# The residual's input moved from GpSimd to VectorE, upward tiles in seven banks, and a new order of the first mixers

## The reference

```python
# first block, 2 layers; mod = silu(c) @ ada_w + ada_b gives shift, scale, gate for each of 3 steps
y = swiglu(modulate(x, shift, scale), w13, w2)                # D_FF = 2816
x = layer_norm(ALPHA * x + 0.5 * (1 + gate) * y, g, b)
y = token_mixer(modulate(x, ...), w_in, w_out, ...)           # gated delta rule, MoBA attention, mLSTM
x = layer_norm(ALPHA * x + (1 + gate) * y, g, b)
y = swiglu(...)                                               # a second feed-forward
x = layer_norm(...)
# second block, 2 layers
y = hybrid mixer(x)       # differential attention, bidirectional HGRN2, attention over a memory
x = layer_norm(alpha * x + y)
y = feed-forward with a convolution of width 3 over the tokens before its gate
x = layer_norm(alpha * x + y)
```

## Time and profile before

| | |
|---|---|
| median of 3 runs | 2046.53 us |
| the profiled execution | 2047.77 us |
| its span, first to last instruction | 2045.9 us |
| TensorE busy | 1977.9 us, 97% |
| VectorE busy | 1580.9 us, 77% |
| ScalarE busy | 1050.9 us, 51% |
| GpSimd busy | 302.4 us, 15% |
| mean granted TensorE clock | 0.995 |
| read from memory | 404 MB, 199 GB/s over the span |

### The profile page before, as it was taken

The page is one execution under the profiler, slowest core; times in us unless marked ns, Lnnn a source line. Parts: engine busy times, 40 slices in busy tenths (PEclk is TensorE's granted clock), DMA queues, the critical chain, the costliest instruction groups (busy, mean ns, idle before and its releaser), DMA issues.

```text
span 2045.9 us, 39790 instructions
## 1 busy us (share of the span) xinstructions
PE 1977.9 (97%) x17036; PEld 1836.6 (90%) x17036; DVE 1580.9 (77%) x2078; ACT 1050.9 (51%) x1451; POOL 302.4 (15%) x255
## 2 busy tenths in 40 slices
PE   7999999999999999999999999999999999999998
PEld 7999889989998998889889989887899899878996
DVE  6699898676987787787676649986798489858974
ACT  4544365545434543554554436665666375746652
POOL 0200031012000200302021002710110027001100
PEclk9999999999999999999999999999999999999999
DMA  9889832235995788422255662342455533334552
GB/s 379 338 339 371 335 117 91 104 125 205 350 345 223 259 338 339 165 103 84 105 192 218 250 235 108 132 157 89 159 207 185 206 137 134 125 109 164 218 192 81
DMA packets 60096, 409.88 MB, mean 200 GB/s; under 512 B 6865, under 2 KB 6865, under 8 KB 13329
## 3 DMA queue, kind: packets, MB, share of 16 engines
q1 hardware_dynamic: 53712, 384.85, 50.5%
q0 software_dynamic: 5920, 22.07, 3.2%
q10 hardware_dynamic: 288, 0.42, 0.1%
HBM read 404.17 MB, written 3.15 MB: 199 GB/s over the span
## 4 chain that ended last, share of the span: by engine, by line
PE 70%; DVE 17%; ACT 5%; issue 3%; POOL 3%; DMA 2%; POOLq 0%; DVEq 0%; SPq 0%; ACTq 0%
PE ps L764 11%; PE ps L766 11%; PE ps L765 11%; PE ps L823 7%; PE ps L825 6%; PE ps L824 6%; DVE l L646 6%; PE ps L1820 2%; PE ps L808 2%; ACT h L631 2%; PE ps L670 2%; PE ps L809 2%; PE ps L810 2%; DMA w<-in_stream 2%; PE ps L883 1%
## 5 line engine op out<-in xcount | busy, mean ns | idle before, releaser
L646 DVE TENSOR_TENSOR l<-w,h 128x2048 fp32r<-128x2048 f32 (+1 forms) x293 | 682.9, 2335 | 127.2 <-ACT h L631 126.8
L631 ACT CAST h<-w 128x2048 fp32r<-128x2048 f32 (+1 forms) x293 | 555.7, 1902 | 343.0 <-PE ps L825 145.9
L764 PE MATMUL ps<-xh,h 128*128 128x256 f32 x2368 | 667.6, 282 | 12.9 <-DVE sa L1469 6.3
L765 PE MATMUL ps<-xl,h 128*128 128x256 f32 x2368 | 659.8, 279 | 0.0
L766 PE MATMUL ps<-xh,l 128*128 128x256 f32 x2368 | 659.7, 279 | 0.0
L764 PEld LDWEIGHTS ps<-xh,h 128*128 128x128 f32 x2368 | 447.9, 189 | 20.5 <-issue 10.1
L765 PEld LDWEIGHTS ps<-xl,h 128*128 128x128 f32 x2368 | 447.0, 189 | 2.2 <-issue 2.2
L766 PEld LDWEIGHTS ps<-xh,l 128*128 128x128 f32 x2368 | 447.0, 189 | 0.0
L823 PE MATMUL ps<-h,hh 128*128 128x512 f32 x528 | 207.0, 392 | 0.0
L824 PE MATMUL ps<-l,hh 128*128 128x512 f32 x528 | 205.5, 389 | 0.0
L825 PE MATMUL ps<-h,hl 128*128 128x512 f32 x528 | 205.5, 389 | 0.0
(11 more groups left out here) (435 smaller groups left out, 3154.8 us busy)
## 6 DMA issues: line engine op xcount, KB each, us to landing
w<-in_stream SPq DMA_DIRECT2D x363, 1024.0 KB, 5.0
GB<-in_vec POOLq DMA_DIRECT2D x20, 512.0 KB, 5.9
gate<-in_vec POOLq DMA_DIRECT2D x6, 512.0 KB, 4.1
w<-in_stream SPq DMA_DIRECT2D x4, 512.0 KB, 4.8
memf<-in_memT SPq DMA_DIRECT2D x2, 512.0 KB, 5.3
xf<-in_xT POOLq DMA_DIRECT2D x1, 1024.0 KB, 10.0
kv<-mk POOLq DMA_DIRECT2D x2, 512.0 KB, 4.7
kv<-mv POOLq DMA_DIRECT2D x2, 512.0 KB, 8.2
```

The lines of the kernel that those rows point to most:

```text
L631: e.copy(part(k.H, m, z), k.W[n % NW][:, 0:z]).then_inc(k.hi_done, 1)
L646: e.tensor_tensor(part(k.L, m, z), k.W[n % NW][:, 0:z], part(k.H, m, z), SUB).then_inc(k.lo_done, 1)
L764: p.matmul(P[:, 0:T], H[:, r, o], xh[:, r, :], start=r == 0, stop=False)
L765: p.matmul(P[:, 0:T], H[:, r, o], xl[:, r, :], start=False, stop=False)
```

## The change

It has four parts.

1. **The residual's input.** `pool_x` is gone, and VectorE makes all of them with `dve_x`: 28 operations more on VectorE, 28 fewer on GpSimd. In the feed-forwards one operation follows each of the upward chunks 5 to 8 of the stage; in `mix1` a new letter `x` in VectorE's string places them. Whoever reads the result now waits on VectorE's semaphore.
2. **New strings** `ORDER1` for TensorE, VectorE and ScalarE in the first mixers, and one wait more on TensorE for GpSimd's `psel` in MoBA.
3. **Seven banks.** Upward tiles of the feed-forwards go round banks 0, 1, 2, 4, 5, 6, 7 after the first four, whose banks depend on the stage before. Bank 3 stays for the sums of the modulation weights. The downward products wait for up to seven banks. In the second mixers the `h` group goes round four banks, 4, 5, 7, 6.
4. **The third chunk's lower part first.** In `ffn2` the call before the loop asks for one chunk more.

```diff
+UPS = (0, 1, 2, 4, 5, 6, 7)
...
     def x_done(self, s):
-        return (self.lv if STAGES[s + 1][0] == "mix2" else self.lg)(s, "x_in", 3)
+        return self.lv(s, "x_in", 3)
...
             if kind in ("ffn1", "ffn2"):
+                lead = (0, 1, 2, 3) if STAGES[s - 1][0] in ("mix1", "mix2") else (0, 1, 6, 7)
                 for u in range(4 * NC2):
-                    self.tile_bank[first + u] = 3 if u == 3 else u % 3
+                    self.tile_bank[first + u] = lead[u] if u < 4 else UPS[u % 7]
...
-def pool_x(k, g, s):
...
-    k.freed.update({k.tile_bank[pe.t - n]: k.evac[pe.t - n] for n in (3, 2, 1)})
+    k.freed.update({k.tile_bank[pe.t - n]: k.evac[pe.t - n] for n in range(7, 0, -1)})
...
 def dve_ffn1(k, v, s, feed):
-    F = ffn_at(s)
+    F, x_in = ffn_at(s), dve_x(k, v, s)
...
         dve_ada(k, v, m)
+        if s > 1 and m in ups(s)[4:8]:
+            next(x_in)
...
 def dve_ffn2(k, v, s, feed):
-    feed.lo(ups(s)[0] + 1)
+    x_in = dve_x(k, v, s)
+    feed.lo(ups(s)[0] + 2)
...
+        if m in ups(s)[4:8]:
+            next(x_in)
...
 ORDER1 = dict(
-    dve=("twrr tww t trr trrw t tggwgg tgw t t t t trw twgbggr t tggggwgbgb t tgggb tgggwgggbbb tgggw t tw tgmg tmggbbgg "
...
+    dve=("t twwrrxw tx trrwrr t txxg tgw t trg tgg tw tw tgwbggr t t tg tgggwgggbbgb tgg tgggwggbb tgw tg tbwggg tmg "
...
+    p.wait_ge(*k.rg(l, "psel", 2))
...
-    interleave(ORDER1["dve"], t=each(tile, tiles1(l)), w=more(feed.lo, feed, ORDER1["dve"].count("w")), r=dve_rows(k, v, l), g=dve_gdn(k, v, l),
+    interleave(ORDER1["dve"], x=dve_x(k, v, s), t=each(tile, tiles1(l)), w=more(feed.lo, feed, ORDER1["dve"].count("w")), r=dve_rows(k, v, l), g=dve_gdn(k, v, l),
...
+HMIX, DMIX = (4, 5, 7, 6), (7, 6)
...
-    pe_mix(k, p, l, k.ho, (4, 5), hv_(l, "on", 3), hp, hv_, 4, keep=7)
+    pe_mix(k, p, l, k.ho, HMIX, hv_(l, "on", 3), hp, hv_, 4, keep=7)
```

More of the change, by code:

```diff
@@ L507, in norm_steps @@
             if not last:
-                (self.lv if STAGES[s + 1][0] == "mix2" else self.lg).add(s, x_in=4)
+                self.lv.add(s, x_in=4)
     def down_table(self):
@@ L1103, in pool_norm @@
             g.tensor_tensor(k.XL[:, 2 * i:2 * i + 2, :], k.tmp[:, i % 3, :, :], k.XH[:, 2 * i:2 * i + 2, :], SUB).then_inc(lg.sem, 1)
-RESID = 4
-def pool_x(k, g, s):
[L1111 to L1124, removed]
 def dve_x(k, v, s):
@@ L1607 @@
 ORDER1 = dict(
-    pe=("tr t t t trr t trgrrrr tgg t t tg t tggg tgb t tggbb tggg tg tbgggb tgbgggggg tggb tbg tbgmg t tmgggg tggmgg "
-        "tg tggmg t tgmg tmgg tmgmmmmgggboomm"),
-    dve=("twrr tww t trr trrw t tggwgg tgw t t t t trw twgbggr t tggggwgbgb t tgggb tgggwgggbbb tgggw t tw tgmg tmggbbgg "
-        "tgwgwg t tgmgg tgwm tgggg tgm tgwgwgmggbmmmmmwmwm t"),
-    act=("twwr t trr trrrw t tw trrgw tg tgw t tg t tgw tggg t t tgwgbgbwggggg t tbgggbgwg tggbwgb tggbg tb tbggw tgggw "
-        "tgmwgg tmgmg tmmggwg tgm tmmgmgw tgggg t tgwgbmmmwm"),
+    pe=("r trr t t trr t t tgrrr tg tg t t t tggg tgbg t tggbb tggggg t tbg tgggbggbgg tgb tbgg tgbggmg t tmggg tggmgg "
+        "tgg tggm t tgmg tmggg tgmmmmggoobmmm"),
+    dve=("t twwrrxw tx trrwrr t txxg tgw t trg tgg tw tw tgwbggr t t tg tgggwgggbbgb tgg tgggwggbb tgw tg tbwggg tmg "
+        "tmgggwggbg t tg tm t t twgmwgggggbgmwggwgmgggmmbm tmmwmwm t"),
+    act=("tww t tr trrwrr trrw t trgw t tggw t tg t tgw tgg tgggw tb t twgggb tgggbgggwg tgbbgwgbb tgg tg tbbggwgg tgwg "
+        "tgwggm tgmmggmm tg tgmmmw tgg tmwggggg t tgwgbmwmmm"),
 )
@@ L2867, in dve_hgrn @@
     yield
-    dve_mix(k, v, l, (4, 5), ha, hv_, k.mixh2, k.mixl2, k.htmp, 4, lambda i: k.COL[:, ROW["hnorm"] + l:ROW["hnorm"] + l + 1], 4)
+    dve_mix(k, v, l, HMIX, ha, hv_, k.mixh2, k.mixl2, k.htmp, 4, lambda i: k.COL[:, ROW["hnorm"] + l:ROW["hnorm"] + l + 1], 4)
     yield
@@ L2921, in act_hgrn @@
     e.wait_ge(k.tile_pe, TILE[FIRST["win2", l, MIX2[-1]] + 1])
-    act_mix(k, e, l, (4, 5), hp, ha, k.mixh2, 4, lambda i: k.COL[:, ROW["hnorm"] + l:ROW["hnorm"] + l + 1], 4)
+    act_mix(k, e, l, HMIX, hp, ha, k.mixh2, 4, lambda i: k.COL[:, ROW["hnorm"] + l:ROW["hnorm"] + l + 1], 4)
     yield
@@ L3017, in pe_diff @@
     yield
-    pe_mix(k, p, l, k.do, (7, 6), dv_(l, "on", 1), dp, dv_, 4, keep=18)
+    pe_mix(k, p, l, k.do, DMIX, dv_(l, "on", 1), dp, dv_, 4, keep=18)
     yield
@@ L3104, in dve_diff @@
     yield
-    dve_mix(k, v, l, (7, 6), da, dv_, k.mixh2, k.mixl2, k.dtmp, 0, lambda i: k.COL[:, ROW["dnorm"] + l:ROW["dnorm"] + l + 1], 4)
+    dve_mix(k, v, l, DMIX, da, dv_, k.mixh2, k.mixl2, k.dtmp, 0, lambda i: k.COL[:, ROW["dnorm"] + l:ROW["dnorm"] + l + 1], 4)
     yield
@@ L3163, in act_diff @@
     e.wait_ge(k.tile_pe, TILE[FIRST["win2", l, MIX2[-1]] + 1])
[L3164 removed]
+    act_mix(k, e, l, DMIX, dp, da, k.mixh2, 0, lambda i: k.COL[:, ROW["dnorm"] + l:ROW["dnorm"] + l + 1], 4)
     yield
```

4 lines of the change are left out of this document (removed).

## The result

The changed kernel takes 2038.66 us (median of 9 runs, 2032.08 to 2044.83) against 2049.28 us (9 runs, 2044.29 to 2054.34) of the kernel before beside it: a ratio of 0.9944, 95% interval 0.9927 to 0.9961. That is 0.56% or some 11 us less; forecast were 5.2 us less, 2041.3 us in a range of 2034.0 to 2048.5. (The forecast started from a median of 2046.5 us of three runs; the nine beside the changed kernel give 2049.3.) Run again later it gave 0.9947 (0.9924 to 0.9970). The profiled execution took 2037.63 us, its span 2035.8 us, with a clock of 0.997.

What follows compares the result with a forecast made beforehand. TensorE, busy 1977.9 of 2045.9 us, was taken as the bound. Terms +2.2 (first mixers), -2.6 (ffn2), -2.8 (pace), -1.2 (s3), -0.8 (second mixers) sum to -5.2 us: 2041.3 us against 2046.5, range 2034 to 2048.5.

Steps and rivals of the forecast that it cites:

- First mixers: +1.1 each: s2 and s5: low clock +1.7 less the Dk wait 0.6 makes each slower by 1.1 us, +2.2 together.
- Behind `RB`: First mixers: a gap up to 5.4 us at RB, then low clock costing 1.7 us; the Dk wait of 0.6 goes.
- the balance of -0.03: First mixers: VectorE's savings and added operations ahead of RB nearly cancel, so RB stays at 292.0 us.
- `Dk` went as forecast: First mixers: TensorE's wait for Dk, 0.6 us each, goes.
- `ffn2`: -1.3 each: s8 and s10: bank waits go, TensorE runs 1.2 to 1.3 us ahead, then meets lower parts; -2.6 us together.
- Pace: -2.8: Slow matmul stretches in s8 and s10 cost 5.6 us; drawn anew, half of that is won.
- the fast pace everywhere: Rival, chance 0.12: the other half of the 5.6 us and s1's slow stretch also go, -5.2 more, 2036.1 us.
- s3: -1.2: s3: the wait for gate, 1.2 us, goes because VectorE gets back 2.15 us shortly before.
- Second mixers: -0.8: s7 and s9: four banks remove the htmp waits, but TensorE then waits for epp; -0.8 us for both.
- overloaded in `ffn2`: Rival, chance 0.11: four x operations per stage make lower parts late and stall TensorE; 2055.7 us, likelier 2051.
- the gains turn into waits for lower parts: Rival, chance 0.20: VectorE's order limits ffn2 and s3, their terms and the pace are 0; 2047.9 us, half 2044.5.
- The mixers gain too: Rival, chance 0.18: no low clock behind RB and RB sooner; first mixers -0.6 to -4.3 us each, 2030.5 to 2038.

Runs made afterwards that it cites:

- a_pool: Changed kernel with the residual's input back on GpSimd in all stages, letters x gone from VectorE's string: 1.0006 of the kernel before.
- a_nofill: Changed kernel without the filler of 48 products in each first mixer: 0.9954 of the kernel before.
- a_poolffn: Changed kernel with the residual's input back on GpSimd in the feed-forwards only: 0.9974 of the kernel before.
- a_banks3: Changed kernel with the feed-forwards' upward tiles in three banks again: 0.9952 of the kernel before.
- a_hmix2: Changed kernel with two banks again for the h group of the second mixers: 0.9959 of the kernel before.
- a_break: Changed kernel with one useless product behind each upward chunk of ffn2 from the fifth on: 0.9951 of the kernel before.
- b_banks7_lo: Kernel before with seven banks in the feed-forwards and the third lower part first in ffn2, nothing else: 0.9988 of the kernel before.
- b_dvex: Kernel before with the residual's input on VectorE in all stages, letters x in the old string and the psel wait: 1.0004 of the kernel before.
- a_again: Changed kernel run again unaltered in a later batch: 0.9947 of the kernel before.

## Why the prediction was right, and where it was not

**The time.** 2038.7 us lies in the range, on its lower side; the gain is twice the forecast. That it lies in the range is in part luck and the range's width: the first mixers' term had the wrong sign, 6.7 us off in both together, that of `ffn2` was too small by half, and those of s3 and of the second mixers did not come.

**First mixers: +1.1 each was forecast, -2.0 to -2.5 each came.** The step that failed is "Behind `RB`": a gap of up to 5.4 us with the low clock after it. In its place the runs showed a gap of 1.4 us there and no fall of the clock. The step itself exists: `a_pool` shows the fall behind a gap of 3.8 us, `a_nofill` the fall and its 1.7 us behind 6.6 us. What was wrong were the two arrivals. The end of the filler came 3.1 us earlier in the stage (filler from 872.19 before and 868.89 after, with the stage's start 0.2 us apart), not the 4.8 us that 3.1 and 1.7 make, because ScalarE's `A` still holds the bank of the third chunk's first tile (1.44 us), a wait that had been hidden behind the lower part's. And the balance of -0.03 failed: `RB` came 2.3 us earlier, 1.6 of it from the locked `A` operation that I had not counted. So the wait for `RB` became 0.6 + 3.1 - 2.3 = 1.4 us. I had looked for GpSimd's effect in the long instructions alone, and a short one can lose as much. That the wait would move to `RB` and not vanish was right, with 1.4 us instead of 3 to 5. `Dk` went as forecast.

**`ffn2`: -1.3 each forecast, -2.4 came.** In the seven profiles that have all four parts in `ffn2` and no more than one interruption in it, s8 takes 187.4 or 190.0 us and s10 182.7 or 185.2, as the last 67 us of the upward tiles are fast or slow: 2.6 us, worked out and measured (67 x 0.038). Before, with both slow, they took 192.4 and 187.7. So 2.4 us each are waits (before, 3.2 us in each stage behind `sa`), the rest of the 5.0 is the draw. The mechanism was named, VectorE's lower parts, but the end of the lock was set against the new operations as if it were only a cover; it was the gain itself: 4.1 to 5.0 us of waits for lower parts come back in s8 with GpSimd's operations (`a_poolffn`, `a_pool`), and three banks cost nothing that could be measured (`a_banks3`).

**Pace: -2.8.** In the profile the slow stretches of the feed-forwards' upward tiles fell from 288 to 161 us, worth 4.8 us, which looks like the other rival ("the fast pace everywhere") half come true. But the second profile of the same kernel has 422 us of them. Probably it largely averages out in the medians: the mixers' 4.5 us and the waits of `ffn2`, 4.8, make 9.3 of the 11 us without it. With s1 it accounts for the distance between the two profiles, and probably for much of the runs' spread of over 12 us. A term that is drawn belongs into the range, not into the sum. Two readings behind the term were rough: the counts in a window include products cut by its edges, so that 112.4 and 116.7 ns are 113.3 and 117.8 from start to start, and the slow stretch at the end of s8 is 67.6 us, not 76.

**s3: -1.2 forecast, none.** The wait for `gate` was 2.2, 2.6 and in other runs 0.3 to 3.2 us. The DMA share from 540 to 590 us is above 0.9 before and after, and the sums `acc` follow the chunks as they come; that faster VectorE work waits there for the stream fits this, but no run tests it. Where the wait was 2.8 and 3.2 us (`a_hmix2`, `a_break`), the clock fell to 0.50 as well and s3 took 198.3 us. **Second mixers: -0.8 forecast, none:** the wait went over to `epp` whole (3.1 for 3.4 us), so VectorE's chain was the limit entirely. In the profile s7 and s9 even take 1.3 and 0.8 us more. In s7 there is a wait of 1.8 us for `pp` that was 0.2 before; in `a_hmix2` it is 0.4 and s7 takes 205.0 us. Whether the four banks cause it is not shown.

**The rivals.** VectorE was not overloaded in `ffn2`: it is busy 116.1 of 130 us in s8, as before, and lower parts are late there once, by 0.3 us. That the gains turn into waits for lower parts is what `b_banks7_lo` shows where GpSimd keeps its work. "The mixers gain too", given 0.18, is what happened, by 2.0 to 2.5 us each, with both of its conditions: no low clock, and `RB` sooner. That the new strings, the banks and the third lower part pay without the move is refuted by `a_pool` (1.0006); that the move pays without them, by `b_dvex` (1.0004, with the letters where I put them). As far as these runs can measure, the gain needs both.

## What to carry to other kernels

Where GpSimd and VectorE both work on SBUF, price a GpSimd operation by what it takes from VectorE, short instructions included, and not by its own busy time: here 28 operations that nobody waited for cost 31 us of VectorE's time. Giving them back to GpSimd in the new order costs the kernel 0.62% or some 12.7 us; taking them away in the old order brought nothing, so the freed time has to be put where somebody waits. Where a wait names a bank, ask why its reader is late before adding banks; four and seven banks brought nothing that could be measured. And try to move work that nobody waits for behind the row operations that somebody waits for: that, with one row operation of ScalarE moved ahead, took another 1.2 to 1.5 us off each mixer.

## What the runs showed of the hardware

The products of 256 columns run at 113.3 or at 117.8 ns at the full clock, for tens of microseconds on end. Which one is drawn when the stream of products starts after a pause and holds until the next: the 113 us from the start of s6 were slow in 8 of 12 profiles without interruption there, and the stage took 201.9 instead of 197.4 us. A single product of another kind between two tiles ended all seven slow stretches that it met in three kernels, and made one of 47 fast ones slow. What the slow pace is, no run here shows.

The length of a gap alone does not tell whether the clock falls. It stayed at 1.00 behind 1.4 us (s2 and s5), 2.6 us (s3 of `a_again`) and 3.3 us (s0 before), and was near 0.5 behind 2.2 us (`a_poolffn`), 2.8 us (`a_hmix2`), 3.1 us (before), 3.8 us (`a_pool`) and 6.6 us (`a_nofill`).

Operations of VectorE on SBUF took up to 2.2 us longer beside one of GpSimd's, long or short: a lower part 4.50 instead of 2.28 us, one on 32 x 256 elements 1.90 instead of 0.28, a copy 2.07 instead of 0.28. Those that read PSUM did not: six on `gq` took 2.94 us in `a_pool` with GpSimd at work, and two groups of three take 3.0 without. GpSimd's own operations took up to 4.46 us instead of 2.40.
